# Last merge and post-norm in PSUM, last slabs ordered by token block, and GpSimd remainders in four pieces

## What is computed

```python
# first block, per layer
merged = (g[:, :, 0] * (o_a @ w_br_mla[l])
          + g[:, :, 1] * (o_b @ w_br_gla[l])
          + g[:, :, 2] * (o_c @ w_br_s5[l]))
x = x + merged @ w_out[l]
h2 = rms_norm(x, norm2_g[l])
x = x + jnp.square(jax.nn.relu(h2 @ w_ff1[l])) @ w_ff2[l]
# second block
merged = jax.nn.sigmoid(z_ga) * y_attn + jax.nn.sigmoid(z_gc) * y_conv
x = x + rms_norm_2(merged @ w_mix_out[l], g_post_mix[l])
h = rms_norm_2(x, g_pre_ffn[l])
x = x + rms_norm_2(swiglu_ffn(h, w_ffn_in[l], w_ffn_out[l]), g_post_ffn[l])
```

## Time and profile before

| | us |
|---|---|
| median of 3 runs (lowest to highest) | 1705.97 (1702.9 to 1707.27) |
| the profiled execution, its device time | 1702.08 |
| its span in the trace | 1700.3 |
| PE busy | 1560.7 (92% of the span) |
| POOL busy | 710.7 (42%) |
| DVE busy | 905.3 (53%) |
| ACT busy | 602.8 (35%) |
| TensorE clock granted, mean | 0.948 of full |

### The profile page before, as it was taken

One profiled execution on the slowest core, in us unless ns is written; L12 is line 12 of the kernel. 1 busy time (PEld: TensorE's weight loads), 2 busy tenths in 40 slices (PEclk: granted clock), 3 DMA queues, 4 the chain that ended last, 5 costly groups with the idle time before them and its releaser, 6 DMA issues.

```text
span 1700.3 us, 22267 instructions
## 1 busy us (share of the span) xinstructions
PE 1560.7 (92%) x9087; PEld 1350.0 (79%) x9087; DVE 905.3 (53%) x1380; ACT 602.8 (35%) x920; POOL 710.7 (42%) x290
## 2 busy tenths in 40 slices
PE   6988889879999999889888899998999999879997
PEld 5876667668889788767666788888999988679996
DVE  2889533533334468982344255533897533356553
ACT  2110241234444311115114433445444552354444
POOL 0000000036988500000001578886888430559995
PEclk9999997989999999989798899999999999989999
DMA  5544332234666465333132456764666332436663
GB/s 144 143 126 102 99 86 74 75 111 138 189 190 191 124 158 137 99 83 106 50 111 79 132 170 191 232 196 138 188 189 189 115 113 86 149 112 189 189 192 126
DMA packets 331679, 234.37 MB, mean 138 GB/s; under 512 B 20222, under 2 KB 315545, under 8 KB 331576
## 3 DMA queue, kind: packets, MB, share of 16 engines
q1 hardware_dynamic: 331576, 232.94, 47.8%
HBM read 231.82 MB, written 1.09 MB: 137 GB/s over the span
## 4 chain that ended last, share of the span: by engine, by line
PE 74%; DVE 13%; issue 4%; ACT 4%; POOL 3%; DMA 1%; SPq 1%; POOLq 0%; DVEq 0%; ACTq 0%
PE ps L1837 18%; PE ps L604 16%; DVE WK L1471 7%; PE ps L964 5%; PE ps L966 5%; PE ps L965 5%; PE ps L1820 3%; PE ps L1822 3%; PE ps L1821 3%; DVE WK L1613 2%; POOL w_lo L1213 2%; PE ps L981 2%; PE ps L1862 2%; PE ps L1049 1%; PE ps L1086 1%
## 5 line engine op out<-in xcount | busy, mean ns | idle before, releaser
L1213 POOL TENSOR_TENSOR w_lo<-raw,w_hi 128x1024 fp32r<-128x1024 f32 x144 | 359.9, 2514 | 796.3 <-ACT w_hi L1247 795.7
L669 POOL TENSOR_TENSOR w_lo<-raw,w_hi 128x1024 fp32r<-128x1024 f32 x142 | 350.6, 2484 | 180.4 <-ACT w_hi L691 172.1
L1837 PE MATMUL ps<-hN,raw 128*128 128x256 f32 (+1 forms) x1376 | 317.7, 392 | 4.5 <-DMA raw<-in_w_in_dram 4.5
L1837 PEld LDWEIGHTS ps<-hN,raw 128*128 128x128 f32 (+1 forms) x1376 | 268.4, 197 | 53.6 <-issue 9.3
L964 PE MATMUL ps<-h_hi,w_hi 128*128 128x256 f32 x800 | 226.8, 284 | 2.4 <-DVE h_lo L838 1.8
L965 PE MATMUL ps<-h_lo,w_hi 128*128 128x256 f32 x800 | 225.0, 281 | 0.0
L966 PE MATMUL ps<-h_hi,w_lo 128*128 128x256 f32 x800 | 224.8, 281 | 0.0
L1247 ACT ACTIVATE w_hi<-raw 128x1024 fp32r<-128x1024 f32 x144 | 152.6, 1060 | 203.4 <-PE ps L604 77.7
L691 ACT ACTIVATE w_hi<-raw 128x1024 fp32r<-128x1024 f32 x142 | 149.6, 1058 | 122.3 <-PE ps L966 33.6
L964 PEld LDWEIGHTS ps<-h_hi,w_hi 128*128 128x128 f32 x800 | 152.1, 190 | 4.0 <-issue 3.5
L966 PEld LDWEIGHTS ps<-h_hi,w_lo 128*128 128x128 f32 x800 | 152.2, 190 | 0.0
(11 more groups left out here) (286 smaller groups left out, 2450.8 us busy)
## 6 DMA issues: line engine op xcount, KB each, us to landing
raw<-in_w_in_dram SPq DMA_DIRECT2D x160, 512.0 KB, 3.8
raw<-in_w_ff_dram SPq DMA_DIRECT2D x128, 512.0 KB, 4.1
raw<-in_w_ffn_in_dram SPq DMA_DIRECT2D x44, 512.0 KB, 3.9
raw<-in_w_ffn_out_dram SPq DMA_DIRECT2D x22, 512.0 KB, 3.6
raw<-in_w_out_dram SPq DMA_DIRECT2D x16, 512.0 KB, 3.6
raw<-in_w_br_s_dram SPq DMA_DIRECT2D x8, 512.0 KB, 3.5
raw<-in_w_br_gla_dram SPq DMA_DIRECT2D x8, 512.0 KB, 3.4
raw<-in_w_br_mla_dram SPq DMA_DIRECT2D x8, 512.0 KB, 3.4
```

Of the source, the lines that this page charges most:

```text
L669: nc.gpsimd.tensor_tensor(out=w_lo[i % RING][:, 0:kt * n], in0=raw[i % RING][:, 0:kt * n], in1=w_hi[i % RING][:, 0:kt * n], op=ALU.subtrac ...
L1213: nc.gpsimd.tensor_tensor(out=w_lo[i % RING][:, 0:kt * n], in0=raw[i % RING][:, 0:kt * n], in1=w_hi[i % RING][:, 0:kt * n], op=ALU.subtract)\
L1837: last = MM(out, w[:, k, c0:c0 + n], x[:, x0 + k, :], start=k == 0, stop=k == kt - 1)
```

## The change

Five things. (1) `merged`: the last merge works in place in PSUM banks 4 to 7, so `G` is only read, and ACT and DVE read the merged pieces from PSUM. The remainder `h_lo` of a piece comes after the next piece's merge. (2) `projection` writes banks 0 to 3 (`ps_out`) and waits for `evac` (banks 0 to 2 read) instead of for the merge's reads. Its first five slabs go as before, the last three go by token block: block 0 with slabs 5, 6, 7, then block 1 with the same three. The last down chunk of each feed-forward does the same with its two slabs. (3) The post-norms work in place in PSUM. (4) Each remainder is made in four POOL operations of 128x256 (`LO_PARTS = 4`). An up product waits only for the quarter that its next two k-tiles need. Down products, projections and SP wait for all four. (5) ACT's copies of the first two up slabs move to between the norms of block 0 and block 1.

```diff
+    LO_PARTS = 4
+        def ps_out(i):
+            return ps[:, 512 * i:512 * i + 512]
-        lo_done = sig("lo_done", SPN[NS], 1)
+        lo_done = sig("lo_done", LO_PARTS * SPN[NS], 1)
-        def merged_piece(dve, tt, l, g, other, p):
-
-            tt(piece(g, p), piece(g, p), piece(other, p), ALU.add).then_inc(hf_ok.s, 1)
-            dve.wait_ge(mh_ok.s, mh_ok(l, p + 1))
-            tt(piece(h_lo, p), piece(g, p), piece(h_hi, p), ALU.subtract).then_inc(ml_ok.s, 1)
+        def merged(dve, tt, stt, l, first_slab, g, other, at):
+
+            for p in range(NP + 1):
+                if p < NP:
+                    dve.wait_ge(used.s, used(l, first_slab + p + 1))
+                    stt(ps_piece(p), piece(g, p), 1.0, ps_piece(p), ALU.add, ALU.mult).then_inc(mg_ok.s, 1)
+                    dve.wait_ge(mg_ok.s, mg_ok(l, at + p + 1))
+                    tt(ps_piece(p), ps_piece(p), piece(other, p), ALU.add).then_inc(hf_ok.s, 1)
+                if p:
+                    dve.wait_ge(mh_ok.s, mh_ok(l, p))
+                    tt(piece(h_lo, p - 1), ps_piece(p - 1), piece(h_hi, p - 1), ALU.subtract).then_inc(ml_ok.s, 1)
...
+        def projection(pe, MM, l, weights):
+
+            for k in range(KD - RING):
+                w = weights(k)
+                if k % 2 == 0:
+                    pe.wait_ge(ml_ok.s, ml_ok(l, k // 2 + 1))
+                by_rows(MM, l, w, h_hi, h_lo, k, k == 0, False, ps_out)
+            pe.wait_ge(ml_ok.s, ml_ok(l, NP))
+            for b in range(NT):
+                for k in range(KD - RING, KD):
+                    by_rows(MM, l, weights(k), h_hi, h_lo, k, False, k == KD - 1, ps_out, (b,))
...
-                    sp.wait_ge(lo_done.s, lo_done(L, SPN2[max(j + 1, 0)]))
+                    sp.wait_ge(lo_done.s, lo_done(L, LO_PARTS * SPN2[max(j + 1, 0)]))
...
-                nc.gpsimd.tensor_tensor(out=w_lo[i % RING][:, 0:kt * n], in0=raw[i % RING][:, 0:kt * n],
-                                        in1=w_hi[i % RING][:, 0:kt * n], op=ALU.subtract).then_inc(lo_done.s, 1)
+                for part in range(LO_PARTS):
+                    cc = slice(kt * n // LO_PARTS * part, kt * n // LO_PARTS * (part + 1))
+                    nc.gpsimd.tensor_tensor(out=w_lo[i % RING][:, cc], in0=raw[i % RING][:, cc],
+                                            in1=w_hi[i % RING][:, cc], op=ALU.subtract).then_inc(lo_done.s, 1)
...
-                    stt(tok(sqt, i), ps_tok(i), nt[:, 16 + b:17 + b], gp[:, k - 1, 512 * (i % 2):512 * (i % 2) + 512],
+                    y = ps_out(i) if k == 1 else ps_tok(i)
+                    stt(y, y, nt[:, 16 + b:17 + b], gp[:, k - 1, 512 * (i % 2):512 * (i % 2) + 512],
                         ALU.mult, ALU.mult).then_inc(post_pr.s, 1)
                     dve.wait_ge(post_pr.s, 4 * (k - 1) + i + 1)
-                    tt(tok(xt, i), tok(xt, i), tok(sqt, i), ALU.add).then_inc(post_ok.s, 1)
+                    tt(tok(xt, i), tok(xt, i), y, ALU.add).then_inc(post_ok.s, 1)
...
             def product(i, out, c0, x_hi, x_lo, fresh=None):
-                wh, wl = weights(i)
                 kt = SL2[i][2]
                 for k in range(kt):
+                    if k % 2 == 0:
+                        wh, wl = weights(i, k // 2 + 1)
...
-                prep(I_FF + 1)
+                prep(I_FF)
                 for b in range(NT):
                     norm_rows(act, A_, l, 1, b, lambda i: (x_mid.s, x_mid(l, i + 1)))
-                prep(I_FF + 2)
+                    prep(I_FF + 2)
...
-                    stt(tok(xt, i), ps_tok(i), 0.5, tok(xt, i), ALU.mult, ALU.add).then_inc(x_mid.s, 1)
+                    stt(tok(xt, i), ps_out(i), 0.5, tok(xt, i), ALU.mult, ALU.add).then_inc(x_mid.s, 1)
...
-            pe.wait_ge(mg_ok.s, mg_ok(L, NP))
...
+            pe.wait_ge(evac.s, evac(L, V_FF))
+            projection(pe, MM, L, lambda k: weights(J_MO + k))
...
-                    for k in range(2):
-                        down(MM, l, weights(l, down_at(c) + k), c % 2, k, c == 0 and k == 0, c == NCH - 1 and k == 1)
+                    for blocks in (((0, 1),) if c < NCH - 1 else ((0,), (1,))):
+                        for k in range(2):
+                            down(MM, l, weights(l, down_at(c) + k), c % 2, k, c == 0 and k == 0,
+                                 c == NCH - 1 and k == 1, blocks)
```

More of the change, by code:

```diff
@@ L603, in by_rows @@
                     for h in range(2):
-                        last = MM(ps_tok(2 * b + h), x[:, k, tb], y[:, 512 * h:512 * h + 512],
+                        last = MM(out(2 * b + h), x[:, k, tb], y[:, 512 * h:512 * h + 512],
                                   start=first_k and n == 0, stop=last_k and n == 2, skip_group_check=True)
@@ L727, in post_norm @@
                     c = slice(16 + b, 17 + b)
-                    link(A_(sqt[:, b, :], ps_half(b), ACT.Square, accum_out=nt[:, c]))
+                    link(A_(sqt[:, b, :], ps_half(k, b), ACT.Square, accum_out=nt[:, c]))
                     link(A_(nt[:, c], nt[:, c], ACT.Ln, scale=1.0 / DM, bias=C("eps4" if k == 1 else "eps")))
                     A_(nt[:, c], nt[:, c], ACT.Exp, scale=-0.5).then_inc(post_rs.s, 1)
+                    if b == 0:
+                        prep(slab + 3)
             pre_norm(1)
@@ L806, in act_second @@
             for p in range(NP):
[L807 removed]
+                merged_hi(act, A_, L, NP, p)
                 prep(J_MO + p + 1)
[L809 removed]
+            prep(J_FF)
             post_norm(1, J_FF - 1)
[L811 removed]
             pre_norm(2)
@@ L937, in dve_second @@
             dve.wait_ge(co_ok.s, 1)
-            for p in range(NP):
-                dve.wait_ge(used.s, used(L, J_AO + p + 1))
-                stt(piece(g, p), piece(g, p), 1.0, ps_piece(p), ALU.add, ALU.mult).then_inc(mg_ok.s, 1)
-                dve.wait_ge(mg_ok.s, mg_ok(L, p + 1))
-                merged_piece(dve, tt, L, g, gc, p)
+            merged(dve, tt, stt, L, J_AO, g, gc, 0)
             dve.wait_ge(gp_in.s, 32)
@@ L1117, in pe_second @@
                 pe.wait_ge(ff2_ok.s, c + 1)
-                for k in range(2):
-                    wh, wl = weights(down2_at(c) + k)
-                    down(MM, L, (wh, wl), c % 2, k, c == 0 and k == 0, c == NC2 - 1 and k == 1)
+                for blocks in (((0, 1),) if c < NC2 - 1 else ((0,), (1,))):
+                    for k in range(2):
+                        down(MM, L, weights(down2_at(c) + k), c % 2, k, c == 0 and k == 0,
+                             c == NC2 - 1 and k == 1, blocks)
         def y_take(dve, l, g, stt):
@@ L1212, in _ @@
                     pool.wait_ge(used.s, used(l, max(i - RING + 1, 0)))
-                    nc.gpsimd.tensor_tensor(out=w_lo[i % RING][:, 0:kt * n], in0=raw[i % RING][:, 0:kt * n],
-                                            in1=w_hi[i % RING][:, 0:kt * n], op=ALU.subtract)\
-                      .then_inc(lo_done.s, 1)
+                    for part in range(LO_PARTS):
+                        cc = slice(kt * n // LO_PARTS * part, kt * n // LO_PARTS * (part + 1))
+                        nc.gpsimd.tensor_tensor(out=w_lo[i % RING][:, cc], in0=raw[i % RING][:, cc],
+                                                in1=w_hi[i % RING][:, cc], op=ALU.subtract).then_inc(lo_done.s, 1)
             pool_second(pool)
@@ L1772, in _ @@
                 dve.wait_ge(gates_t.s, gates_t(l, 2))
-                merge(0)
+                merged(dve, tt, stt, l, I_BRA, G[:, 0:KD, :], G[:, KD:2 * KD, :], 2 * NP)
                 for i in range(4):
@@ L2123, in _ @@
                 branch(I_BRA, o)
-                for k in range(KD):
-                    w = weights(l, I_OUT + k)
-                    if k == 0:
-                        pe.wait_ge(mg_ok.s, mg_ok(l, 3 * NP))
-                    if k % 2 == 0:
-                        pe.wait_ge(ml_ok.s, ml_ok(l, k // 2 + 1))
-                    by_rows(MM, l, w, h_hi, h_lo, k, k == 0, k == KD - 1)
+                pe.wait_ge(evac.s, evac(l, U_FF))
+                projection(pe, MM, l, lambda k: weights(l, I_OUT + k))
                 x_to_h(pe, l, 1, 0)
```

48 lines of the change are left out of this document (20 added, 28 removed).

## The result

The changed kernel takes 1758.1 us (median of 4 runs, 1745.6 to 1770.4) against 1705.7 (4 runs, 1702.9 to 1707.3): ratio 1.031, 95% interval 1.023 to 1.038. The forecast was 1772, slower. The sign, the place and the bound were right. The size was near for a partly wrong reason: POOL's fixed cost is 0.14 us and not 0.20, which is worth some 39 us less, and a wait of VectorE that I had not foreseen brought most of that back. That the two errors nearly cancel is luck.

What follows compares the result with a forecast made beforehand. PE set the pace with POOL close behind; four pieces would make POOL the bound. From 1702.1 us, +82 - 7 - 5 - 4 gave 1768, and 3.9 for the median over the profiled run made 1772 us; range 1700 to 1838.

Steps and rivals of the forecast that it cites:

- The fixed cost, 0.20 us: Each extra POOL operation costs a fixed a = 0.20 us, so a slab takes POOL 2.97 us instead of 2.37.
- Layers +51: Feed-forwards of both layers: POOL needs 12.98 us a chunk, 1.71 more than 11.27, for 15 full chunks each: +51 us.
- Second feed-forward +24: Second block's feed-forward: POOL needs 19.36 us a chunk, 2.44 more, for 10 chunks: +24 us.
- `w_in` +7: Second block's `w_in` products: POOL needs 0.14 us more a slab, for 48 slabs: +7 us.
- Layer merges 7: Layers' merge and projection: merge runs free, block 0's norm goes under block 1's matmuls; 3.5 us a layer, 7 saved.
- Second block 5: Second block's projection: first post-norm goes under block 1's matmuls and the projection ends sooner; 5 us saved.
- Last chunks 4: Last down chunks: block 0 done half a slab pair earlier, 1.4 us at three places; 4 us saved.
- Part 5 at nothing: Two ACT copies between the norms fill time spent waiting for block 1: no cost, or 2 us a layer without cover.
- Overlap (a under 0.06): Rival: POOL's fixed cost a stays under 0.06 us an operation, PE keeps the pace everywhere; 1690 us, chance 0.14.
- the even case: Rival: a between 0.06 and 0.10 us, losses of 0 to 20 us meet the 16 gained; about 1706 us, chance 0.06.
- The clock rival: Rival: PE waits in every slab and its granted clock falls; 1809 us, chance 0.10.
- Merge savings don't come: Rival: POOL paces the projection and takes the merge savings; 16 us more, 1788 us, part of the POOL-bound case.

Runs made afterwards that it cites:

- after_again: The changed kernel measured again with no edit: 1754.9 us, ratio 1.028 to the kernel before.
- pieces_only: The kernel before with only the four POOL pieces a remainder and the quarter waits: 1758.9 us, ratio 1.033.
- psum_ff_four: The changed kernel, still four pieces, with the feed-forwards' DVE operations in place in PSUM: 1695.3 us, ratio 0.994 to the kernel before.
- rest_one_piece: The changed kernel with LO_PARTS = 1, each remainder one POOL operation of 1024 columns: 1683.6 us, ratio 0.989 to the kernel before.

## Why the prediction was right, and where its terms were off

- **POOL becomes the bound: right.** PE is at 92 to 95% in the three stretches, POOL at 93% and above, and the chunks take 4 x 2.79 + 1.10. The remainders start 0.70 us apart; 0.74 was named as right and under 0.65 as wrong. A steady layer chunk takes 12.2 us, not 13, and PE waits less than the 10 to 15% that went with 13.
- **The fixed cost, 0.20 us: mis-sized.** It is 0.14, alone and in the kernel. DVE's estimate (0.15) had been the better row; I took ACT's because POOL is slower, and that argument was empty: the slowness lies in the columns. With 0.14 the three terms are 29.7 + 13.6 + 0 = 43 us, not 82, and the forecast would have been 1733.
- **The three terms against the trace.** Layers +51: measured 25.7 + 16.0 = 41.7. Second feed-forward +24: 16.0. `w_in` +7: the 48 slabs took about 1 us more here, and 2 to 5 in after_again, pieces_only and psum_ff_four. Of the layers' 41.7 some 28 are rate by an estimate (30 chunks of 12.21 instead of 11.27), the rest long waits less the last chunks' gain; no run separates them. The prediction also took layer two for a second layer one. It is not: there the kernel before has chunks of up to 15.72 us, and its feed-forward takes 192.1 us against 183.3, so the pieces add 16.0 there and 25.7 in layer one.
- **Missing: the long waits.** The prediction tacitly took DVE's delay beside a remainder for bounded by the piece's length. The pieces were made shorter, and single delays became longer: up to 27 us where nothing before was over 2.83. The prediction's sentence on SBUF — State Buffer, of the Trainium skill, a pair that is locked for one instruction, bounds a wait by one piece; the trace differs, with 13.78 us over some 20 pieces, and it decides. In the first trace the long waits give 13.0 us in the convolution and, as an estimate from the pairs of chunks in pieces_only, some 3.5 us for each of five over 8 us in the layers, next to nothing in the second feed-forward: about 30 us, where a forecast of 1733 would have been 25 too low.
- **The savings: right in sum, by another split.** Layer merges 7: measured 4.1 + 3.6. But the prediction had most of it behind the projection, from block 0's norm, and only 1.3 us at the projection's end, which it put at 391 us in the kernel before; that is where its window ends, and the last matmul ends at 392.7. In layer one 3.8 of the 4.1 us are at the projection's end (27.5 us after the last branch instead of 31.3) and 0.3 in the norm (6.1 instead of 6.5), and pieces_only reaches 27.6 too. Second block 5: 6.3. Last chunks 4: at the end 1.4 us; in the layers they are within the feed-forward's loss and not shown apart. Alone (rest_one_piece) the whole is 19 us by the medians and 12 by the spans, against 16.
- **Part 5 at nothing: wrong.** Its cover was named as ACT's time; the price was DVE's, by way of two remainders that came earlier: 1.7 us a layer with one piece (8.2 against 6.5). With four pieces, as in the changed kernel, the gap is 6.1 us, so there no net price shows.
- **The sum of the parts.** The pieces alone cost 56 us and the rest alone gives 19, which makes 37; together they cost 52. By the spans it is 52.1 - 12.2 = 39.9 against 58.0, so 18 us apart. The table shows 10.5 of them: the pieces alone already shorten the three merges by 3.7, 3.1 and 3.7 us, since DVE gets in after 0.7 us instead of 2.4, and that gain can't be had twice. Another 10.9 are the second block up to its last branch (313.0 against 302.1), where the convolution's wait lies in this execution; the other stages give 3 back.
- **The rivals.** Overlap (a under 0.06) and the even case fell with the spacing. The clock rival was right in kind: after waits of 4 us PE ran at the lower clock, 0.97 in the mean, where I had named below 1.00 as a sign against me. What it cost is not shown apart. "Merge savings don't come" fell.
